# Two stacked model blocks on one core: the order of small work on VectorE, ScalarE and TensorE around an attention loop

## The reference

```python
x = first_block(x, positions, ...)              # 2 layers, then rmsnorm
o_c, o_s, o_w = compressed, selected, windowed attention, causal
y = concat(rms_norm(y_nsa), rms_norm(y_gmlp), rms_norm(y_conv))
x = x + y @ w_out
x = x + memory_cross_attention(x, mem, ...)     # needs mem @ wk and mem @ wv
x = x + conv_ffn(x, ...)
return rms_norm(x, final_norm_g)
```

## Time and profile before

| | us |
|---|---|
| median of 3 runs | 2635.04 (2633.44 to 2638.72) |
| the profiled execution, its own time | 2637.93 |
| its span | 2636.1 |
| PE busy | 2542.3 (96% of the span) |
| DVE busy | 1237.7 (47%) |
| ACT busy | 907.2 (34%) |
| POOL busy | 1252.6 (48%) |
| mean granted clock of PE | 0.979 |

### The profile page before, as it was taken

One profiled execution on the slowest core, in us unless ns is written; L12 is line 12 of the kernel. 1 busy time (PEld: TensorE's weight loads), 2 busy tenths in 40 slices (PEclk: granted clock), 3 DMA queues, 4 the chain that ended last, 5 costly groups with the idle time before them and its releaser, 6 DMA issues.

```text
span 2636.1 us, 34492 instructions
## 1 busy us (share of the span) xinstructions
PE 2542.3 (96%) x11696; PEld 2056.3 (78%) x11696; DVE 1237.7 (47%) x1471; ACT 907.2 (34%) x1281; POOL 1252.6 (48%) x879
## 2 busy tenths in 40 slices
PE   8999999999999999999999999999777799999998
PEld 6887788888888888877888888888644487888887
DVE  5434612452322543451245332268776654788373
ACT  4223433332222422343333222243345433444233
POOL 4554355555555555534555554555322142555454
PEclk8999999999999999999999999999888899999999
DMA  4333133333333333323333333363111031333332
GB/s 146 100 95 88 56 96 96 97 95 98 99 96 98 93 101 96 92 59 88 96 96 96 96 96 97 102 152 89 57 48 41 25 95 48 96 96 96 98 99 74
DMA packets 448120, 236.23 MB, mean 90 GB/s; under 512 B 16144, under 2 KB 442256, under 8 KB 447888
## 3 DMA queue, kind: packets, MB, share of 16 engines
q1 hardware_dynamic: 446896, 232.38, 30.6%
q10 hardware_dynamic: 1120, 2.51, 0.3%
HBM read 232.76 MB, written 2.10 MB: 89 GB/s over the span
## 4 chain that ended last, share of the span: by engine, by line
PE 89%; DVE 6%; issue 2%; ACT 1%; POOL 1%; DMA 0%; DVEq 0%; ACTq 0%; POOLq 0%
PE unit_ps L1673 58%; PE unit_ps L1794 16%; PE unit_ps L1780 7%; PE aux L1708 2%; PE o_banks L1738 1%; DVE a_f L1342 1%; DVE row L1328 1%; PE unit_ps L1933 1%; DVE c_f L1215 1%; PE aux L1726 1%; POOL wl L422 1%; PE o_banks L1919 1%; PE aux L2009 1%; DVE aux L1326 0%; PE unit_ps L1708 0%
## 5 line engine op out<-in xcount | busy, mean ns | idle before, releaser
L422 POOL TENSOR_TENSOR wl<-raw,wh 128x512 fp32r<-128x512 f32 x862 | 1246.1, 1466 | 1363.4 <-ACT wh L504 853.3
L504 ACT ACTIVATE wh<-raw 128x1024 fp32r<-128x1024 f32 x304 | 322.3, 1061 | 1028.1 <-PE unit_ps L1673 975.3
L1673 PE MATMUL unit_ps<-ah,wh 128*128 128x512 f32 x1280 | 503.5, 393 | 3.6 <-DVE tmp L1072 3.6
L1673 PE MATMUL unit_ps<-al,wh 128*128 128x512 f32 x1280 | 499.5, 390 | 0.0
L1673 PE MATMUL unit_ps<-ah,wl 128*128 128x512 f32 x1280 | 499.5, 390 | 0.0
L1673 PE MATMUL unit_ps<-bh,wh 128*128 128x512 f32 x768 | 299.7, 390 | 0.0
L1673 PE MATMUL unit_ps<-bl,wh 128*128 128x512 f32 x768 | 298.8, 389 | 0.0
L1673 PE MATMUL unit_ps<-bh,wl 128*128 128x512 f32 x768 | 298.8, 389 | 0.0
L1673 PEld LDWEIGHTS unit_ps<-ah,wh 128*128 128x128 f32 x1280 | 241.2, 188 | 55.9 <-DVE tmp L1072 4.4
L1673 PEld LDWEIGHTS unit_ps<-al,wh 128*128 128x128 f32 x1280 | 240.9, 188 | 51.4 <-issue 1.9
L1673 PEld LDWEIGHTS unit_ps<-ah,wl 128*128 128x128 f32 x1280 | 241.1, 188 | 50.5
(11 more groups left out here) (349 smaller groups left out, 3876.6 us busy)
## 6 DMA issues: line engine op xcount, KB each, us to landing
raw<-w_in_dram SPq DMA_DIRECT2D x147, 512.0 KB, 4.0
raw<-w_up_dram SPq DMA_DIRECT2D x64, 512.0 KB, 4.0
raw<-w_down_dram SPq DMA_DIRECT2D x64, 512.0 KB, 4.0
raw<-up_dram SPq DMA_DIRECT2D x44, 512.0 KB, 3.8
raw<-w_conv_out_dram SPq DMA_DIRECT2D x16, 512.0 KB, 4.0
raw<-w_ret_out_dram SPq DMA_DIRECT2D x16, 512.0 KB, 3.9
raw<-w_o_dram SPq DMA_DIRECT2D x16, 512.0 KB, 4.0
raw<-down_dram SPq DMA_DIRECT2D x16, 512.0 KB, 3.8
```

The source lines that it names most:

```text
L422: last = pool.tensor_tensor(wl[j][:, half], raw[j % 2][:, half], wh[j][:, half].bitcast(F32), ALU.subtract)
L504: act.activation(wh[j][:], raw[j % 2][:], ACT.Copy).then_inc(w_hi, 1)
L1673: last = pe.matmul(unit_ps[j % 2][:], w[j][:, k], v[:, k * T:(k + 1) * T], start=(k == 0 and n == 0), stop=(k == KB - 1 and n == 2))
```

## The change

- ACT makes the sines after the square root of layer 0, behind the splits of units 4 to 7, instead of ahead of the layer loop. That loop is now unrolled on ACT. A wait for `ones_set` that had been met before goes.
- PE does the gated mixing's matmuls ahead of the last query unit instead of behind it. DVE's sum and product on the mixing go ahead of `z_query(3)`, in the place of two convolution sums, which are made later.
- In the attention loop PE transposes the first two blocks of step k - 1 (`first_turns`) ahead of the memory unit; the wait for `p_ready` goes with them, the wait for `o_taken` stays with the values, behind the memory unit. In `values` the transposes run two ahead of the value matmuls.
- ACT copies the first two transposed blocks beside the first two exponentials, ahead of the memory unit's copy.
- DVE does `take_out` ahead of `shift` and `weigh` in its step.
- `CV_STEP` goes from 7 to 9, so that the convolution's sums end at step 8; the reciprocal of `rstd_x` moves from step 12 to step 7 and the two `first_norm` steps from 13 and 14 to 14 and 15.

```diff
-GM_STEP, CV_STEP = 3, 7
+GM_STEP, CV_STEP, TAPS_IN_STEP = 3, 9, 3
# ACT, start
-            act.wait_ge(ang_done, 1)
-            act.activation(sin[:], sin[:], ACT.Sin).then_inc(trig_done, 1)
-            act.activation(cos[:], cos[:], ACT.Sin).then_inc(trig_done, 1)
-            act.wait_ge(ones_set, 1)
...
-            with act.Fori(0, LAYERS) as l:
+            for l in range(LAYERS):
...
                     if f == 3:
                         sqrt_ms(l * 2 + 1)
+                        if l == 0:
+                            act.wait_ge(ang_done, 1)
+                            act.activation(sin[:], sin[:], ACT.Sin).then_inc(trig_done, 1)
+                            act.activation(cos[:], cos[:], ACT.Sin).then_inc(trig_done, 1)
# ACT, attention loop
-                if more:
-                    exp_head(k + 1, 0)
-                    exp_head(k + 1, 1)
+                turns = turns_of(k - 1)
+                for n in range(2):
+                    if n < len(turns):
+                        take_turn(*turns[n])
+                    if more:
+                        exp_head(k + 1, n)
                 mem_copy(k)
                 ahead2(MK + k)
-                turns = turns_of(k - 1)
-                for n in range(max(len(turns), 2)):
-                    if n < len(turns):
-                        take_turn(*turns[n])
-                    if more and n < 2:
-                        exp_head(k + 1, 2 + n)
+                for turn in turns[2:3]:
+                    take_turn(*turn)
+                if more:
+                    exp_head(k + 1, 2)
+                for turn in turns[3:4]:
+                    take_turn(*turn)
+                if more:
+                    exp_head(k + 1, 3)
+                for turn in turns[4:]:
+                    take_turn(*turn)
# DVE, ahead of the loop (the same four operations go from behind z_query(3))
-            some_taps(2)
+            dve.wait_ge(mix_mm, 2)
+            for i in range(2):
+                go()
+                biased = tmp[1][:].rearrange("p (c t) -> p c t", c=NC)
+                did(dve.tensor_tensor(biased, o_ps[i]..., gm_bias[:, i]..., ALU.add))
+                mult(y_gm[i], gm_u[i], tmp[1][:], mixed)
             z_query(3)
# DVE, norms
-                elif k == CV_STEP + 5:
+                elif k == CV_STEP - 2:
                     go()
                     did(dve.reciprocal(rstd_x, rstd_x))
-                if k in (CV_STEP + 6, CV_STEP + 7):
+                if k in (CV_STEP + 5, CV_STEP + 6):
# DVE, attention loop
                 mixer_norms_first(k)
+                if b == 1 and it:
+                    take_out(it - 1)
...
                 weigh(k)
-                if b == 1 and it:
-                    take_out(it - 1)
-                some_taps(3)
+                some_taps(TAPS_IN_STEP)
                 mixer_norms_last(k)
# PE
-            for f in range(Z_KW, Z_Q + 4):
+            for f in range(Z_KW, Z_Q + 3):
                 z(f)
...
+            def first_turns(k):
+                it, b, c, rp = STEPS2[k]
+                if b == 0:
+                    pe.wait_ge(pc_ready, 1)
+                pe.wait_ge(p_ready, k + 1)
+                for j in turns_of(k)[:2]:
+                    turn_block(j)
+
             def values(k):
                 it, b, c, rp = STEPS2[k]
-                mine = [j for j, turn in enumerate(TURNS) if turn[0] == k]
-                pe.wait_ge(p_ready, k + 1)
-                if b == 0:
-                    pe.wait_ge(pc_ready, 1)
-                    if it:
-                        pe.wait_ge(o_taken, it)
+                if b == 0 and it:
+                    pe.wait_ge(o_taken, it)
+                mine = turns_of(k)
                 for j in mine:
-                    turn_block(j)
-                    if j > mine[0]:
-                        block_values(j - 1)
-                block_values(mine[-1])
+                    block_values(j)
+                    if j + 2 <= mine[-1]:
+                        turn_block(j + 2)
...
+            z(Z_Q + 3)
             pe.wait_ge(evac, U2 + NZ + 2)
...
-                mem_unit(k)
                 if k == 0:
                     pe.wait_ge(shift_cmp, 1)
                 else:
+                    first_turns(k - 1)
+                mem_unit(k)
+                if k:
                     values(k - 1)
+            first_turns(N_STEPS - 1)
             values(N_STEPS - 1)
```

More of the change, by code:

```diff
@@ L1314, in _ @@
             z_query(2)
-            some_taps(2)
+            dve.wait_ge(mix_mm, 2)
+            for i in range(2):
+                go()
+                biased = tmp[1][:].rearrange("p (c t) -> p c t", c=NC)
+                did(dve.tensor_tensor(biased, o_ps[i].rearrange("p (c t) -> p c t", c=NC), gm_bias[:, i].unsqueeze(1).broadcast_to([P, NC, P]), ALU.add))
+                mult(y_gm[i], gm_u[i], tmp[1][:], mixed)
             z_query(3)
@@ L1376, in compressed_weights @@
                 mult(p_cmp, p_cmp, by_head.unsqueeze(3).broadcast_to([P, 2, NC * REP, N_CMP]), pc_ready)
[L1378 to L1383, removed]
             shift(0, 0)
@@ L1430, in mixer_norms_last @@
                     did(dve.reciprocal(part_r[2], part_r[2]))
-                elif k == CV_STEP + 5:
+                elif k == CV_STEP - 2:
                     go()
                     did(dve.reciprocal(rstd_x, rstd_x))
-                if k in (CV_STEP + 6, CV_STEP + 7):
+                if k in (CV_STEP + 5, CV_STEP + 6):
                     for n in range(4):
-                        first_norm(4 * (k - CV_STEP - 6) + n)
+                        first_norm(4 * (k - CV_STEP - 5) + n)
             def take_out(it):
@@ L1935, in block_values, with turns_of @@
                         last.then_inc(o_att, 1)
+            def turns_of(k):
+                return [j for j, turn in enumerate(TURNS) if turn[0] == k]
+            def first_turns(k):
[5 more added lines that the diff above has]
+                    turn_block(j)
             def values(k):
                 it, b, c, rp = STEPS2[k]
-                mine = [j for j, turn in enumerate(TURNS) if turn[0] == k]
-                pe.wait_ge(p_ready, k + 1)
-                if b == 0:
-                    pe.wait_ge(pc_ready, 1)
-                    if it:
-                        pe.wait_ge(o_taken, it)
+                if b == 0 and it:
+                    pe.wait_ge(o_taken, it)
+                mine = turns_of(k)
                 for j in mine:
-                    turn_block(j)
-                    if j > mine[0]:
-                        block_values(j - 1)
-                block_values(mine[-1])
+                    block_values(j)
+                    if j + 2 <= mine[-1]:
+                        turn_block(j + 2)
             pe.wait_ge(gm_ready, 1)
```

## The result

| | before | after |
|---|---|---|
| median of the runs | 2634.24 (2632.62 to 2638.72, 4 runs) | 2595.45 (2593.16 to 2598.61, 4 runs) |
| the profiled execution, its own time | 2637.93 | 2597.18 |
| its span | 2636.1 | 2595.4 |
| mean granted clock of PE | 0.979 | 0.985 |

The ratio is 0.9853, 95% interval [0.9841, 0.9866]: 38.8 us faster by the medians. Forecast was 2589 (2576 to 2607), so the time lies 6.4 us above it and inside the range.

The account below looks back on a forecast made before the run. Slack was seen only at the start and in the second block's attention loop, where engines wait for each other in turn; PE is busy between. Gains 8.8 + 5.7 + 31.3 = 45.8 us gave 2589 us, range 2576 to 2607.

Parts of the forecast that it names:

- Part 1: Start: sines moved behind the root let weight splits and root come sooner; 8.8 us gained, bounds 3 and 10.5.
- the drain: Start, ACT table switches: the skill's drain of about 1.38 us each would leave 7.4 us; rejected from the trace.
- Part 2: Before the attention loop: gated mixing ahead of the last query unit, 64 compressed-score matmuls in 3.45 us; 5.7 us gained.
- Part 3: Second block's attention loop: wait for the copy goes, DVE's work becomes the bound; 31.3 us gained, bounds 15 and 39.
- The handovers: Loop: waits that stay, 4.6 us at step 9 (convolution's sum) and 2.7 at step 11 (Silus, squares); 7.3 us.
- the deduction of 5.5: Loop: taken off the 36.8 us gain, 3.0 for POOL's low parts and 2.5 for PE at half clock.
- The 3.0 us for POOL: Loop: POOL's 15 low parts always fall on DVE work, costing 0.2 us each.
- B: Rival for the loop: only the named wait goes, PE bounds it at clock 0.82; 22.2 us gained, 2598; chance 0.27.
- The signs: Expected in the trace: root near 41 us, first query/key unit near 60, 64 matmuls about 3.5 us, loop near 156.
- C: Rival for the start: raw loads and a long low clock bind it, gaining only 3 us; 2595; chance 0.10.
- D: Rival for the loop: PE's queue waits as long, loop keeps 187 us, only the start counts; 2620; chance 0.03.
- E: Rival for the loop: PE at half clock throughout, 28 us slower overall; 2663; chance 0.03.

Follow-up runs that it names:

- e3: Kernel before the change with only DVE's copy of the head outputs (`take_out`) moved to the front of its step; 2615.19 us, ratio 0.9918.
- e4: Kernel before with only the turns' new order: two transposed blocks ahead of the memory unit, their ACT copies earlier; 2617.57 us, ratio 0.9927.
- e5: Changed kernel with DVE's copy of the head outputs put back behind the weights; 2603.33 us, ratio 0.9880.
- e11: Changed kernel with the first two transposed blocks behind the memory unit on PE and their copies behind its copy on ACT; 2604.25 us, ratio 0.9892.
- e1: Kernel before with only the two sines moved behind the root and ACT's layer loop unrolled; 2627.89 us, ratio 0.9962.
- e8: Changed kernel with the root and the sines one value unit earlier, ahead of the split of unit 7; 2593.67 us, ratio 0.9838.
- e7: Changed kernel with Identity in place of Silu for the two convolution outputs, dropping the table loads around it; 2594.85 us, ratio 0.9848.
- e2: Kernel before with only the gated mixing put ahead of the last query unit and two convolution sums moved into the loop; 2632.48 us, ratio 0.9989.
- e10: Changed kernel with root and sines one unit earlier, and the `rstd_x` reciprocal and eight first norms moved into DVE's z-stage waits; 2586.61 us, ratio 0.9818.
- e9: Changed kernel with the `rstd_x` reciprocal moved from step 7 into a DVE wait of the z stage; 2590.64 us, ratio 0.9837.
- e6: Changed kernel with the convolution's sum and what follows two steps earlier again (`CV_STEP` 7), reciprocal back at step 12; 2597.41 us, ratio 0.9856.
- a1: Changed kernel measured once more, unaltered, for comparison on its chip; 2595.60 us, ratio 0.9852.

## Why the prediction was right, and where its sizes were off

**What bounds the kernel.** Right. The layers gave nothing but the 1.7 us of clock that are told below, and the loop was a ring of engines that wait for each other in turn; e3, e4, e5 and e11 show its links.

**Part 1, 8.8 us, measured 7.0** (7.4 in e1). The chain was as described. Two terms were off. Unit 5's split starts at 29.81 for my 29.0, and the root comes 8.45 us earlier in place of 8.9. And I let PE need the 19.2 us of before for units 4 to 7; it needed 20.7, for it came out of its wait of 4.33 us at half clock and stayed there until 47.5, 6.1 us, where before it had stayed 3.1 us after resuming. With the clock up all along these matmuls take 17.8 us (e8, and e7 with its wait of 3.61 us). This term is one of chance: over the eight traces with this start they took 20.5 to 20.7 us in five, 19.4 in e5 and 17.8 in e7 and e11, and the first query/key unit comes at 58.1 to 62.0 us. My 8.8 lies within that, though not for the reasons given. The detour of the sines was hidden, as said: ACT was done with unit 8's split at 45.38. As to the drain that the Trainium skill gives (ScalarE: Activation LUTs, "What ACT_TABLE_LOAD costs"), the changed kernel agrees with the earlier trace rows against it: the split ends at 39.31 and the load starts at 39.32, with nothing between them. Nor would a drain have lowered the gain to 7.4, as I wrote, since the same load stands ahead of the root before and after.

**Part 2, 5.7 us, measured 4.1** in the pair. The four kernels without this edit have 120.9 to 123.3 us in this stretch, mean 121.8; the eight others that have it, with the new start, 116.7 to 117.4, mean 117.0: 4.8 us. The order came as predicted. The mis-sized term is the 64 matmuls: 4.87 us for my 3.45. At full clock all along they take 3.66 (e2), so half the clock in their last third is 1.2 of the 1.6 that are missing. In e8 and e10 they took 3.66 as well, but there the clock was 0.83 from 1790 to 1800 us and the gated mixing came 1.7 us later behind the last reciprocal, so that their stretch is no shorter.

**Part 3, 31.3 us, measured 29.1**, by the prediction's own cut (step 1 to the end of the last copy). Step by step: DVE's work in steps 1 to 13 was 121.9 us. I had 121.8 and 5.5 for POOL and the clock on top. The handovers I put at 7.3 were 13.7: 0.2 in step 4, 2.2 and 4.1 us in steps 9 and 10, where PE waits 7.6 us for the convolution's sum and then runs at half clock, and 7.2 in front of step 12, where I had 2.7 for Silus and squares and left out the table load behind them (1.5 us with what hangs on it, by e7) and PE's half clock there (2.35, by e9). The end from step 14 on was 22.3 for 21.1. So 121.9 + 13.7 + 22.3 = 157.9 against 155.7: the deduction of 5.5 covered, by luck, most of a loss of another kind: the two parts were mis-sized by 6.4 and 1.2 us.

The 3.0 us for POOL were half there. DVE's forms in steps 1 to 15, before and then after:

```profile
L1215 DVE SCALAR_TENSOR_TENSOR c_f<-hp,vectors,c_f 128x512 f32<-128x512 f32 x23 | 21.9, 954 | 0.8
L1342 DVE TENSOR_SCALAR a_f<-a_f,row 128x128 f32<-128x128 f32 x12 | 7.3, 612 | 0.4
```

```profile
L1221 DVE SCALAR_TENSOR_TENSOR c_f<-hp,vectors,c_f 128x512 f32<-128x512 f32 x25 | 25.3, 1012 | 0.9
L1353 DVE TENSOR_SCALAR a_f<-a_f,row 128x512 f32<-128x512 f32 x16 | 12.4, 777 | 0.6
L1353 DVE TENSOR_SCALAR a_f<-a_f,row 128x128 f32<-128x128 f32 x12 | 5.4, 449 | 0.4
```

The convolution's sums and the largest scalings slowed (954 to 1012 ns; 708 to 777), the smallest scalings went from 612 to 449. In all DVE is busy for 131.0 us of the loop where it was for 127.6; 1.9 of these 3.4 are the two sums, 1.5 are slower forms. And they lie where they cost nothing: DVE's work in steps 14 and 15 took 19.1 us for my 17.4, beside PE's end. That POOL is the cause is not shown.

"Moving the convolution's chain only redistributes" is shown by e6. "The wait for the copy goes, and the ACT copies no longer stall PE's values" is two statements, of 20 us each alone, and 9.4 and 8.0 when the other is in place. I had not split the part so; a reader of the prediction would not have known that either edit alone gives two thirds.

By the rule of the Trainium skill (TensorE: Matmul & The Clock Gate, "What's actually happening") the loop would have been at full clock once PE's gaps go. It was 0.91, and gaps stayed: the clock was 0.50 from 1954 to 1960 us, around the end of the wait for the convolution's sum, and again from 1990 to 1996. That the clock follows PE's activity up holds at the start, where it came back at 47.5 us with PE busy since 41.36; that it fell inside the 64 matmuls, with PE busy, is more than the rule as I used it. Nor does "half clock follows idle of 3 us and more", my argument against B, hold each time: e7 kept full clock behind 3.61 us.

**The signs.** Those named for the start and for the loop came, the first query/key unit 2 us late. The 3.5 us for the 64 matmuls did not. Of the steps 9 to 12, which I gave up to 13 us, step 11 took 13.8 from its scores to the next.

**The rivals.** B (only the named wait goes, PE the bound at clock 0.82, 2598) has nearly the right time and the wrong mechanism: the clock rose, and PE kept 26.4 us of idle. C (2595) has the measured time to half a microsecond, also by luck: its 3 us for the start are out by e1, and its loop of 31.3 was 29.1. D and E are out.

**The whole.** 7.0 + 4.1 + 28.6 and the 1.7 in between are 41.4 for a forecast of 45.8; another 0.7 came back after the loop. The 1.7 were not forecast and are luck, so what the three parts gave is 39.7.

## What to carry to other kernels

Where two engines wait for each other in turn, ask of each link what it is worth alone and what it is worth when the other links are gone: here 20 and 20 made 29. Work that fills another engine's latency (the memory unit between a transpose and its use) was worth here about as much as a wait taken away. Before moving work off an engine, look who sets the end of that stretch: one reciprocal taken from step 7 gave its 3.35 us, eight norms taken from the last two steps nothing. And before a gain is put down to an edit, compare the granted clock of the stretch in both traces: 2.3 us of e9's gain and all of the layers' 1.7 were clock.

## What the runs showed of the hardware that was not expected

- The granted clock fell to half while PE was fully busy, in the 64 matmuls of 31 columns of the changed kernel (1.00, 0.71, 0.50 in three successive microseconds), and did not in the same matmuls of e2. Of the ten traces with this order, seven show the fall (4.87 to 5.23 us for the 64) and e2, e8 and e10 do not (3.66). What tells them apart is open.
- A like wait does not always bring the clock down: at the start it kept its upper level behind a wait of 3.61 us in e7 and fell behind one of 3.51 in a1; ahead of step 12 it fell to 0.51 in the changed kernel and stayed at 1.00 in e9 and e10, with the same waits of PE.
- After a wait of 1.8 us for DVE, once in each layer, the clock falls in some executions and not in others. The windows of before (PE busy, granted clock), and those of after, which have DVE, ACT and POOL as well:

```profile
320.00:330.00 10.00, 8.21 (x36) 0.97 0.18 52
330.00:340.00 10.00, 10.00 (x40) 0.86 0.36 102
```

```profile
320.00:330.00 10.00, 8.21 (x37) 6.52 (x36) 3.33 (x6) 5.73 (x6) 5.09 (x4) 1.00 0.16 48
330.00:340.00 10.00, 10.00 (x46) 8.29 (x45) 1.38 (x2) 4.29 (x5) 5.08 (x4) 1.00 0.45 130
```

The mean clock from 260 to 360 us was 0.98 in all four traces without the new start, and in two of the ten with it (e5, e8); from 1160 to 1260 us it was 0.98 in nine of the fourteen and 1.00 in e2, e4, e5, e7 and e11. From the first query/key unit to the last reciprocal the traces take 1689.0 us with both falls (before, e3), 1687.2 to 1687.4 with one and 1686.0 to 1686.1 with none (e7, e11); e8 and e10, which wait for the keys' rotation, are aside. So the 1.7 us of the table above are one fall less, which e2 and e4 have without the new start: they are not the change's. The start adds its own scatter, 58.1 to 62.0 us for the same code. Together the two explain why e7 and e11 reach the last reciprocal at 1744.2 to 1744.5 and the others with this start at 1747.5 to 1749.3.
